# A decoder layer on eight cores: transposes by DMA, transfers moved, and the last normalisation split over three engines

## The reference, cut to what matters

```
proj = x @ w_in                      # columns: q,k,v,gate of GLA, low-rank decay, q,k,v of the window group
gk   = log_sigmoid(gk_lo @ w_gk2 + b_gk) / 16
gla  = chunked gated linear attention with a state carried over the sequence (4 heads, dk 128, dv 256),
       per-head RMSNorm, times silu(gate)
swa  = sliding-window attention, window 128, 16 query heads of 64 on 2 kv heads, learned sinks
x1   = LN(2**0.25 * x + concat(gla, swa) @ w_out)
out  = LN(2**0.25 * x1 + relu(x1 @ w_up)**2 @ w_down)      # 2048 -> 8192 -> 2048
```

## Time and profile before

| | |
|---|---|
| median of 3 runs | 2822.8 us (2821.64 to 2823.19) |
| profiled execution, its own time | 2822.92 us |
| span of its slowest core (of 2810.8 to 2821.4) | 2821.4 us |
| busy PE, DVE, ACT, POOL | 97%, 36%, 22%, 4% |
| granted clock of TensorE, mean | 0.991 of full |
| DMA, mean | 91 GB/s |

### The profile page before, as it was taken

How to read it: one execution, slowest core, us unless ns; L and a number is a source line. 1 busy time by engine, 2 the same in 40 slices (tenths; PEclk the granted TensorE clock), 3 DMA queues, 4 the chain that set the end, 5 groups by cost and what they waited for, 6 DMA issues and landing times.

```text
span 2821.4 us, 37826 instructions; the slowest of 8 cores (2810.8 to 2821.4 us)
## 1 busy us (share of the span) xinstructions
PE 2726.7 (97%) x14367; PEld 1363.0 (48%) x14608; DVE 1013.9 (36%) x1480; ACT 630.1 (22%) x1347; POOL 125.1 (4%) x227
## 2 busy tenths in 40 slices
PE   6999999999999999999999999999999999999987
PEld 3446674444444444444444676444444444444433
DVE  2553545751211212121257444582211211221138
ACT  3434655331001001001003555332101101100100
POOL 2000000000000000000000000000000000000000
PEclk9999999999999999999999999999999999999998
DMA  9674445635454354445578334734354344335342
GB/s 153 84 122 75 78 89 99 144 78 92 69 88 75 60 90 75 75 69 89 83 121 194 75 63 104 159 81 90 60 90 77 73 74 91 75 60 90 75 75 120
DMA packets 50913, 256.24 MB, mean 91 GB/s; under 512 B 4656, under 2 KB 21552, under 8 KB 22192
## 3 DMA queue, kind: packets, MB, share of 16 engines
q0 software_dynamic: 44400, 211.47, 45.1%
q1 hardware_dynamic: 6336, 42.35, 4.2%
HBM read 448.47 MB, written 16.78 MB: 165 GB/s over the span
## 4 chain that ended last, share of the span: by engine, by line
PE 90%; DVE 4%; issue 2%; ACT 2%; DMA 2%; POOL 0%; DVEq 0%; ACTq 0%; POOLq 0%; SPq 0%
PE ps L292 88%; PE ps L295 1%; DVE racc L323 1%; ACT racc L312 1%; DVE racc L449 1%; DMA rexu<-w_kv 1%; DMA y<-racc 1%; DVE racc L315 0%; DMA wring<-w_down 0%; ACT rext L312 0%; ACT racc L327 0%; DVE rext L315 0%; DVE bnst L967 0%; ACT small L312 0%; DVE rexu L315 0%
## 5 line engine op out<-in xcount | busy, mean ns | idle before, releaser
L292 PE MATMUL ps<-wring,xreg 128*128 128x512 bf16 (+1 forms) x6594 | 1234.8, 346 | 12.2 <-DMA wring<-w_down 7.1
L292 PE MATMUL ps<-xreg,wring 128*128 128x512 bf16 (+1 forms) x5443 | 1200.8, 380 | 14.6 <-ACT racc L312 5.2
L292 PEld LDWEIGHTS ps<-wring,xreg 128*128 128x128 bf16 x6688 | 651.3, 98 | 583.0 <-issue 23.9
L292 PEld LDWEIGHTS ps<-xreg,wring 128*128 128x128 bf16 (+1 forms) x5568 | 539.5, 98 | 654.1 <-issue 21.0
L312 ACT ACTIVATE tmpr<-ps 128x512 f32<-128x512 f32 (+1 forms) x320 | 177.9, 556 | 1407.2 <-PE ps L292 1404.6
L315 DVE TENSOR_TENSOR xreg<-tmpr 128x512 bf16<-128x512 f32 x256 | 177.1, 692 | 705.0 <-ACT tmpr L312 705.0
L315 DVE TENSOR_TENSOR racc<-racc,ps 128x512 f32<-128x512 f32 x240 | 164.8, 687 | 507.9 <-PE ps L292 455.9
L323 DVE SCALAR_TENSOR_TENSOR racc<-racc,ps 128x512 f32<-128x512 f32 x128 | 87.8, 686 | 221.9 <-PE ps L292 221.6
L323 DVE SCALAR_TENSOR_TENSOR racc<-racc,small,rext 128x2048 f32<-128x2048 f32 x64 | 149.5, 2338 | 4.4 <-DVE racc L323 2.0
L292 PE MATMUL ps<-xreg 128*128 128x512 bf16 (+1 forms) x532 | 114.5, 373 | 0.6
L312 ACT ACTIVATE small<-small 128x1 f32<-128x1 f32 x192 | 38.7, 202 | 321.2 <-DVE small L826 312.4
(11 more groups left out here) (94 smaller groups left out, 934.0 us busy)
## 6 DMA issues: line engine op xcount, KB each, us to landing
wring<-w_up POOLq DMA_DIRECT2D x64, 1024.0 KB, 10.1
wring<-w_down POOLq DMA_DIRECT2D x64, 1024.0 KB, 10.0
wring<-w_gla POOLq DMA_DIRECT2D x26, 1024.0 KB, 9.4
racc<-x_own SPq DMA_DIRECT2D x16, 1024.0 KB, 12.6
y<-racc SPq DMA_DIRECT2D x16, 1024.0 KB, 4.2
xreg<-xT_prev POOLq DMA_DIRECT2D x16, 512.0 KB, 32.1
xreg<-xT_own POOLq DMA_DIRECT2D x16, 512.0 KB, 16.2
wring<-w_qs POOLq DMA_DIRECT2D x8, 1024.0 KB, 10.8
```

Source lines behind the costliest of these rows:

```text
L292: P.add("pe", lambda h: h.matmul(out, lhsT=lhsT, rhs=rhs, start=start, stop=stop), [lhsT, rhs], [out])
```

## The change

- 592 of the 784 PE transposes become DMAs with transpose, issued by SP through a helper `dtr` on twelve semaphores in turn: x1T (one DMA for a tile of 128x2048), the gated outputs (128x256), the scaled keys and the window group's values in the passes (128x512), and the token rows of blocks 2 and 3 of the prefix (16 DMAs of 128x512 each). The copies out of PSUM by ACT and DVE go with them. The prefix's blocks 0 and 1 and its keys stay on PE. Block 2's rows go to a place of their own in xreg1.
- `gla_chunks` has eight steps behind its first instead of ten; beside the second query projection only one step takes two chunks instead of three.
- The prefix's halo products and their weights' place move: the weights lie in xreg0 and the products run behind block 1's keys. Block 1's x is issued ahead of these weights, the fourth block's x behind the halo products.
- x of the next pass: three pieces before a quarter of down products instead of two.
- The last pass: the weights of column quarter 2 go to the free x region and are issued before the down products of the last round begin. `ln2_last` takes 1280 columns on DVE and 768 on ACT (scale and shift) and POOL (multiply by and add the affine rows), with two stores a tile.

```diff
@@ -256,17 +256,18 @@
         junk = tmpr_t[:, 0, 0:128].bitcast(BF16)
...
         x1b = [EY[:, i * 2048:(i + 1) * 2048] for i in range(2)]
+        XV = [XR[i][:, :].rearrange("p (k t) -> p k t", k=16) for i in range(2)]
         x_tok = RA[:, 12288:20480].rearrange("p (t e) -> p t e", e=2048)
+        x_tokb = XR[1][:, 0:8192].rearrange("p (t e) -> p t e", e=2048)
         kd_all = [RA[:, 20480 + i * 2048:22528 + i * 2048].rearrange("p (t e) -> p t e", e=512) for i in range(2)]
...
         wg_prev = EY[:, 3072:3584].rearrange("p (k n) -> p k n", n=32)
-        wkv_prev = EX[:, 0:4096].rearrange("p (k n) -> p k n", n=256)
+        wkv_prev = XV[0][:, :, 512:768]
         m_part = [f32v(r, o, 4096).rearrange("p (k e) -> p k e", e=512) for r, o in ((RA, 24576), (EX, 0))]
...
         bbc = f32v(EX, 4096, 2048)
-        XV = [XR[i][:, :].rearrange("p (k t) -> p k t", k=16) for i in range(2)]
         acc = [f32v(RA, t * 4096, 2048) for t in range(8)]
...
         def record(P, wplan):
@@ -377,6 +378,13 @@
                     wrel.add(i)
...
 
+            tctr = [0]
+
+            def dtr(out, in_):
+                i = tctr[0] % 12
+                tctr[0] += 1
+                P.add("sp", lambda h: h.dma_start(out=out, in_=in_, transpose=True), [in_], [out], stream=f"t{i}")
+
             xq = []
...
             def queue_half(src, pi, half, reg, dest):
@@ -413,16 +421,20 @@
 
...
                 wks = [load_w(w_gla[h * 3][:, 0:2048], 16, 128) for h in range(4)]
+                queue_half(xT_prev, 1, 0, 1, 0)
+                issue_x(4)
                 load_piece("c8", wkv_prev, w_kv[:, 0:4096])
-                queue_half(xT_prev, 1, 0, 1, 0)
                 queue_half(xT_prev, 0, 1, 0, 0)
-                queue_half(xT_prev, 0, 0, 0, 1)
-                issue_x(12)
-                dma("pool", "c6", masks_b[:].rearrange("p a b -> p (a b)"), masks, [], [masks_b[:]])
-                wcap[0] = 6
+                issue_x(4)
                 blocks = [XV[1][:, :, 512:1024], XV[1][:, :, 0:512], XV[0][:, :, 0:512], XV[0][:, :, 512:1024]]
 
+                xts = [x_tok, x_tok, x_tokb, x_tok]
+
                 def x_rows(b, kg2):
+                    if b >= 2:
+                        for kc in range(kg2 * 8, kg2 * 8 + 8):
+                            dtr(xts[b][:, :, kc * 128:(kc + 1) * 128], blocks[b][:, kc, :])
+                        return
                     for tq in range(4):
...
                         for j in range(8):
@@ -481,7 +493,7 @@
                     for dc in dcs:
...
                         for t in range(4):
-                            mm(bk[:, :], x_tok[:, t, dc * 128:(dc + 1) * 128], kd_all[b % 2][:, t, :], t == 0, t == 3)
+                            mm(bk[:, :], xts[b][:, t, dc * 128:(dc + 1) * 128], kd_all[b % 2][:, t, :], t == 0, t == 3)
                         mp = m_part[dc // 8][:, dc % 8, :]
...
                             cp("act" if dc % 2 else "dve", mp, bk[:, :])
@@ -493,28 +505,41 @@
                 x_rows(0, 1)
...
                 rows = keys(0)
-                bk = next_bank()
-                for kc in range(16):
-                    mm(bk[:, 0:128], wkv_prev[:, kc, 0:128], blocks[0][:, kc, 384:512], kc == 0, kc == 15)
-                ks_copies(bk, 0, 128)
                 rows(3)
-                bk = next_bank()
-                for kc in range(16):
-                    mm(bk[:, 0:128], blocks[0][:, kc, 384:512], wkv_prev[:, kc, 128:256], kc == 0, kc == 15)
-                cp("act", vs[:, 0, :], bk[:, 0:128])
                 for b in range(4):
...
                     if b < 3:
-                        x_rows(b + 1, 0)
+                        if b == 0:
+                            x_rows(1, 0)
                         gates(b + 1)
                     sums(b, range(8, 16))
+                    if b == 1:
+                        for kg2 in range(2):
+                            x_rows(3, kg2)
                     if b < 3:
                         decays(b + 1)
-                        x_rows(b + 1, 1)
+                        if b == 0:
+                            x_rows(1, 1)
                         keys(b + 1)(3)
                     if b == 0:
+                        bk = next_bank()
+                        for kc in range(16):
+                            mm(bk[:, 0:128], wkv_prev[:, kc, 0:128], blocks[0][:, kc, 384:512], kc == 0, kc == 15)
+                        ks_copies(bk, 0, 128)
+                        bk = next_bank()
+                        for kc in range(16):
+                            mm(bk[:, 0:128], blocks[0][:, kc, 384:512], wkv_prev[:, kc, 128:256], kc == 0, kc == 15)
+                        cp("act", vs[:, 0, :], bk[:, 0:128])
+                        queue_half(xT_prev, 0, 0, 0, 1)
+                        issue_x(4)
+                        dma("pool", "c6", masks_b[:].rearrange("p a b -> p (a b)"), masks, [], [masks_b[:]])
                         for h in range(2):
                             load_piece(f"wo{h}", wv_prev[h], w_gla[h * 3 + 1])
+                        wcap[0] = 6
+                        if wplan is not None:
+                            issue_w()
+                        for kg2 in range(2):
+                            x_rows(2, kg2)
                     if b == 1:
...
                         issue_x(4)
@@ -578,15 +603,12 @@
                         bv = next_bank()
...
                         cp("act", vsT_h[half], bv[:, :])
+                        dtr(vs[:, 1 + half * 4:5 + half * 4, :], vsT_h[half])
                         yield
...
                         yield
-                        bkb = next_bank()[:, :].bitcast(BF16)
-                        for j in range(4):
-                            tr(bkb[:, j * 128:(j + 1) * 128], vsT_h[half][:, j * 128:(j + 1) * 128])
-                        cp("act", vs[:, 1 + half * 4: 5 + half * 4, :], bkb[:, 0:512].rearrange("p (t e) -> p t e", t=4))
                     for half in range(2):
...
                         yield
@@ -601,12 +623,6 @@
                 def gla_proj(h):
...
 
-                    def kd_transposes(half):
-                        bkb = next_bank()[:, :].bitcast(BF16)
-                        for j in range(4):
-                            tr(bkb[:, j * 128:(j + 1) * 128], kdT[half][:, j * 128:(j + 1) * 128])
-                        cp("act", kd_tok[hb][:, half * 4:(half + 1) * 4, :], bkb[:, 0:512].rearrange("p (t d) -> p t d", t=4))
-
                     ki, wkq = load_w(w_gla[h * 3], 32, 128)
...
 
@@ -622,6 +638,7 @@
                             act(tf[:, j * 128:(j + 1) * 128], c_f[:, h, cj * 128:(cj + 1) * 128], AF.Exp,
...
                         tt(kdT[half], bk[:, :], tf, ALU.mult)
+                        dtr(kd_tok[hb][:, half * 4:(half + 1) * 4, :], kdT[half])
 
...
                         bk = next_bank()
@@ -632,7 +649,6 @@
                     k_step(0)
...
                     k_step(1)
-                    kd_transposes(0)
                     yield
...
                         bk = next_bank()
@@ -640,9 +656,7 @@
                         tf = tmpf[half]
...
                         stt(qtT[hb][:, half * 512:(half + 1) * 512], bk[:, :], 128.0 ** -0.5, tf, ALU.mult, ALU.mult)
-                        if half == 0:
-                            kd_transposes(1)
-                        else:
+                        if half == 1:
                             release_w(ki)
...
                     vi, wv = load_w(w_gla[h * 3 + 1], 16, 256)
@@ -686,13 +700,7 @@
                         rs = next_small()
...
                         stt(gla_h[t % 4], bo[:, 0:256], rs, gw[:, t, :], ALU.mult, ALU.mult)
-
-                    def tpose(t):
-                        bkb = next_bank()[:, :].bitcast(BF16)
-                        for ec in range(2):
-                            tr(bkb[:, ec * 128:(ec + 1) * 128], gla_h[t % 4][:, ec * 128:(ec + 1) * 128])
-                        cp("act" if t % 2 else "dve", mixT[:, 2 * h:2 * h + 2, t * 128:(t + 1) * 128],
-                           bkb[:, 0:256].rearrange("p (e t) -> p e t", e=2))
+                        dtr(mixT[:, 2 * h:2 * h + 2, t * 128:(t + 1) * 128], gla_h[t % 4])
 
...
                         bk = next_bank()
@@ -703,11 +711,8 @@
                         tt(At4[half].rearrange("p (c t) -> p c t", c=4), bk[:, :].rearrange("p (c t) -> p c t", c=4),
...
                     yield
-                    for t in range(10):
-                        if t > 1:
-                            tpose(t - 2)
-                        if t < 8:
-                            chunk(t)
+                    for t in range(8):
+                        chunk(t)
                         yield
...
                 def swa_proj(g):
@@ -793,7 +798,7 @@
                 for i in range(8):
...
                     advance(g3)
-                    if i in (2, 4, 6):
+                    if i == 4:
                         advance(g3)
...
                         advance(b1)
@@ -841,18 +846,9 @@
```

(53 more changed lines are left out.)

## The result

| | before | after |
|---|---|---|
| median, same chip | 2822.80 us (2821.64 to 2823.19, 3 runs) | 2847.76 us (2846.15 to 2857.41, 4 runs) |
| ratio | | 1.0093, 95% interval 1.0076 to 1.0111: slower |
| span of the slowest core | 2821.4 us | 2844.6 us (core 5) |
| spans of the eight cores | 2810.8 to 2821.4 | 2806.7 to 2844.6 |
| busy PE, DVE, ACT, POOL | 2726.7, 1013.9, 630.1, 125.1 us | 2715.0, 999.8, 583.1, 163.4 us |

I had forecast 2783 and given "slower" a chance of 0.13.

The account below looks back on a forecast made before the run. PE was taken as the bound, busy 2726.7 of 2821.4 us. Transposes off PE, 28.2, plus the end, 12, gave 40.2 us; 2822.8 less that, rounded, was 2783, forecast range 2775 to 2789 (wider range 2768 to 2812).

Parts of the forecast that it names:

- slower: Rival: transposing DMAs too slow for x1T and prefix, at 1.6 us a block, 3108 us in all; chance 0.13.
- Transposes off PE, 28.2 us: Whole kernel: 592 of 784 transposes leave PE, which shortens its list by 28.2 us net.
- The 2 us for head 3's chunks: Beside the second query projection: fewer double-chunk steps cut PE waits on DVE's gated outputs, between 0 and 7 us, taken as 2.
- waits of 3.2 us before the keys and half a fall of the clock: Prefix blocks 2 and 3: PE's 1.29 us waits behind DVE become 3.2; possible clock falls cost 4.6 us, half taken, 2.3.
- r, the time of a block: Transposing DMAs: time per 128x128 block among many, 2 to 4 us per 16-block tile; covered up to 0.6 us a block.
- A transpose queued behind 1 MB loads: SP's queue: transposes late behind loads, four chunk buffers hiding some 10 us; price 0 to 5 us, 0 in the sum.
- half slow: Rival: 0.5 to 0.75 us a block or transposes stuck in SP's queue, stalls of 5 to 15 us; 2797 to 2818; chance 0.13.
- The prefix's budget: Prefix block 2: 64 blocks to transpose in some 38 us before its sums, covered up to 0.6 us a block.
- The end, 12 us: Last eight tiles: early weights and split normalisation gain 12 us, the middle of cases with and without POOL disturbing DVE.
- POOL holds DVE up: Rival in the end stage: gain there 0 to 6 us in place of 12, total 2789 to 2795; chance 0.22.
- The bound of 8.1 to 9.2 us a tile: End stage: tile time if each tile's DVE chain waits once for a POOL instruction, leaving a gain of 9 to 0 us.
- Moved transfers, 0: Next pass's x, prefix's fourth block and halo products: moving them gains nothing, at most 1 us for x.

## Why the prediction was wrong

- *Transposes off PE, 28.2 us.* Right for what PE saves: keys and gated outputs 11.8 of 12.1; x1T 13.9 of 14.2 on the median core, though only 6.8 on the slowest. The 2 us for head 3's chunks are right by luck as to the reason: the waits they were to come from grew. In the prefix I forecast waits of 3.2 us before the keys and half a fall of the clock; they were 2.90 and 2.96, with a fall behind both (16 products in 4.89 and 4.87 us, where a record of 16 takes 3.62). I had priced one fall in two, at 2.3 us; the two cost 2 x 1.3 = 2.6. So I was wrong on how often the clock falls and on the price of one, and the two nearly cancel.
- *r, the time of a block.* Right as measured alone: 4.3 us for the 16 blocks of a tile (I took 2 to 4), r = 0.27; 2.4 to 2.5 for a DMA of four. It was read off one store that had the DMA engines to itself.
- *"A transpose queued behind 1 MB loads ... Price 0 to 5 us, I take 0".* **This step failed.** I looked at SP's queue, where no weight load stands, and not at what POOL had in flight on the same 16 DMA engines. Beside it tiles of x1T took 10 to 60 us over the runs and prefix DMAs of four blocks up to 41.6. In the prefix this cost 22.6 us in place of a gain of 1.5 (9.5 to 10.7 of it with the pair waits below), and in x1T about 7 of the 14.2 by the slowest core. Keys and gated outputs met loads too, up to 20.3 us, and lost nothing: their buffers (four for the gated outputs, two for the keys) covered it. What decided was the slack, and for x1T (two buffers and a deadline) and the prefix I had compared it with undisturbed transfers. My case "half slow" had the mechanism in it ("stuck behind loads in SP's queue") with the wrong queue, and ended at 2818 since I saw stalls at one place only.
- *The prefix's budget.* "64 blocks in some 38 us" for block 2 would have done without loads: sixteen DMAs 1.3 us apart and 2.5 us for the last are 22 us, an estimate from the first four, which had nothing beside them. The fourth block's x, which the change itself moves beside these DMAs, and two weights made it 41.7 even without the other loads. For block 3 I hadn't looked at how the program tracks `racc`: the pair wait was 9.5 to 10.7 us. I had worked out waits that the change adds on ACT and DVE, not those between its own new DMAs.
- *The end, 12 us.* PE's two waits went as forecast; without the split this gave 9.9. The split was the rival "POOL holds DVE up": I gave it 0 to 6 us, measured 1.7. The bound of 8.1 to 9.2 us a tile held (8.47). Taking the middle of two cases when a rule spoke for one of them cost 10 us of forecast.
- *Adding up.* The sum goes by one chain, but the time is that of the slowest of eight cores. A stall that hits some cores takes its gain from the metric at once, and meets the other losses on the unlucky core: 24 us of the changed kernel's loss are in none of its parts alone, and what the metric doesn't explain of them is open.
- *Moved transfers, 0.* Not tested by themselves.

What stays open: why the two queues slow one another down (the number of small packets, their size or an order among queues; no run varied one of them alone), and why tile 2, beside the same loads, lands after 13.6 us on one core and after 53.2 on another.

## What to carry to other kernels

A DMA that takes work off a busy engine is priced by what else the DMA engines carry at that moment, on every queue: look for loads in the rows of the same microseconds before you take a time from an undisturbed transfer. Put such DMAs where no large load is in flight, or hold the load until they have landed, and look at where the held load goes. Look at all cores: a gain of 14 us on most was 7 by the slowest. Test parts of a change alone, and add them up again: here three gained 7 to 12 us each (x1T, keys with gated outputs, early weights), a small one, 1.5 us in my sum, cost 23, and the whole lost 24 more than its parts.

## What the runs showed of the hardware

- Transposing DMAs of bf16 run as packets of under 512 bytes, some 135 for a 128x128 block. Alone: 16 blocks in 4.2 to 4.4 us (6.1 at most in the run without the loads), 4 blocks in 2.4 to 2.5, SP busy for 1.17 us with an issue of four. Beside loads of 1 MB from POOL's queue: up to 60.0 and 41.6 us, and the loads up to 42.9 (median 8.6).
- SP itself is then stuck in the issue, up to 38.8 us, so whatever stands behind it on SP is late as well.
- Cores of one chip, all on the same program, differ by up to 38 us in such a kernel (2806.7 to 2844.6), where they differed by 11 before. The slowest counts.
- POOL takes 1.27 us for 128x512 float32 with two SBUF inputs. A DVE instruction with two SBUF inputs that starts while one of POOL's runs ends late by about what was left of it (2.90 us in place of 1.54), and the other way round (2.87 in place of 1.80). Evictions from PSUM beside POOL stay at 0.67 us.
